# Who subtracts the low halves of twelve projection slabs: VectorE or GpSimd, with the context keys and values cut into pieces between them

## What is computed

```
hx = rmsnorm(x, g) * (1 + sc_x) + sh_x          # 512 tokens
hc = rmsnorm(ctx, g) * (1 + sc_c) + sh_c        # 256 context tokens
qx = rope(rmsnorm(hx @ wq))                     # 16 heads of 64
kx = rope(rmsnorm(hx @ wk)); vx = hx @ wv       # 4 heads of 64
kc = rmsnorm(hc @ wk);       vc = hc @ wv
p  = softmax(qx @ concat(kx, kc).T / 8);  y = (p @ concat(vx, vc)) @ wo
```

## Time and profile before

| | |
|---|---|
| median of 3 runs | 3340.39 us (3338.66 to 3344.8) |
| span of the profiled execution | 3345.0 us |
| TensorE busy | 3225.9 us, 96% |
| VectorE busy | 1487.9 us, 44% |
| ScalarE busy | 1193.4 us, 36% |
| GpSimd busy | 763.8 us, 23% |
| GpSimd low parts (L2433) | 254 instructions, 568.9 us |
| VectorE low parts (L1212) | 188 instructions, 217.5 us |

### The profile page before, as it was taken

The page is one execution under the profiler, slowest core; times in us unless marked ns, Lnnn a source line. Parts: engine busy times, 40 slices in busy tenths (PEclk is TensorE's granted clock), DMA queues, the critical chain, the costliest instruction groups (busy, mean ns, idle before and its releaser), DMA issues.

```text
span 3345.0 us, 38977 instructions
## 1 busy us (share of the span) xinstructions
PE 3225.9 (96%) x15760; PEld 2474.1 (74%) x15760; DVE 1487.9 (44%) x2166; ACT 1193.4 (36%) x1764; POOL 763.8 (23%) x399
## 2 busy tenths in 40 slices
PE   6999999999999999999999899999999979999998
PEld 4657777777665777777777576888888658868887
DVE  3572243132357114313269746223333899653234
ACT  3443234233344223423331154211112548632223
POOL 4303334434330343434310000000000039500000
PEclk9999999999999999999999999999999989999999
DMA  6413444544340455465335311222222110123322
GB/s 233 124 43 107 145 126 137 163 141 149 115 133 19 128 160 171 148 191 160 125 91 127 84 48 35 70 63 64 63 63 63 38 38 1 35 67 88 108 87 77
DMA packets 429893, 337.23 MB, mean 101 GB/s; under 512 B 16637, under 2 KB 411223, under 8 KB 417428
## 3 DMA queue, kind: packets, MB, share of 16 engines
q1 hardware_dynamic: 428272, 334.23, 32.9%
q0 software_dynamic: 1248, 0.46, 0.1%
q10 hardware_dynamic: 196, 0.07, 0.0%
HBM read 319.58 MB, written 2.10 MB: 96 GB/s over the span
## 4 chain that ended last, share of the span: by engine, by line
PE 59%; DVE 6%; ACT 2%; POOL 1%; issue 1%; SPq 0%; DMA 0%; DVEq 0%; ACTq 0%
PE PS L423 17%; PE PS L424 17%; PE PS L425 17%; PE PS L771 1%; POOL p L2478 1%; PE PS L586 1%; PE PS L512 1%; DVE both_tmp L1289 1%; PE PS L565 1%; PE PS L1075 1%; PE PS L1076 0%; PE PS L1044 0%; PE PS L1055 0%; DVE stat_r L1272 0%; DVE stat_t L1266 0%
## 5 line engine op out<-in xcount | busy, mean ns | idle before, releaser
L423 PE MATMUL PS<-Hh,Wh 128*128 128x512 f32 x2208 | 877.0, 397 | 13.7 <-DVE Hl L1303 9.4
L424 PE MATMUL PS<-Hl,Wh 128*128 128x512 f32 x2208 | 861.8, 390 | 0.0
L425 PE MATMUL PS<-Hh,Wl 128*128 128x512 f32 x2208 | 861.3, 390 | 0.0
L2433 POOL TENSOR_TENSOR Wl<-raw,Wh 128x1024 fp32r<-128x1024 f32 (+2 forms) x254 | 568.9, 2244 | 1099.3 <-ACT Wh L1950 1099.3
L1950 ACT ACTIVATE Wh<-raw 128x1024 fp32r<-128x1024 f32 (+2 forms) x442 | 436.1, 987 | 404.4 <-PE PS L425 394.2
L423 PEld LDWEIGHTS PS<-Hh,Wh 128*128 128x128 f32 x2208 | 416.0, 188 | 139.1 <-issue 74.0
L425 PEld LDWEIGHTS PS<-Hh,Wl 128*128 128x128 f32 x2208 | 415.6, 188 | 87.8
L424 PEld LDWEIGHTS PS<-Hl,Wh 128*128 128x128 f32 x2208 | 416.2, 188 | 67.2 <-issue 3.5
L1212 DVE TENSOR_TENSOR Wl<-raw,Wh 128x1024 fp32r<-128x1024 f32 (+3 forms) x188 | 217.5, 1157 | 386.2 <-ACT Wh L1950 385.7
L1858 DVE SCALAR_TENSOR_TENSOR cv<-PS,vcols,cv 128x510 f32<-128x510 f32 (+1 forms) x176 | 123.7, 745 | 295.7 <-ACT cv L2357 295.7
L423 PE MATMUL PS<-g_h,Wh 128*128 128x512 f32 x528 | 211.2, 400 | 0.0
(11 more groups left out here) (370 smaller groups left out, 4827.0 us busy)
## 6 DMA issues: line engine op xcount, KB each, us to landing
raw<-in_ffn_w SPq DMA_DIRECT2D x108, 512.0 KB, 3.8
mod_w<-in_w_mod SPq DMA_DIRECT2D x48, 1024.0 KB, 5.6
raw<-in_w_up SPq DMA_DIRECT2D x88, 512.0 KB, 3.8
mod_w<-in_w_ada SPq DMA_DIRECT2D x40, 1024.0 KB, 6.0
raw<-in_w_in SPq DMA_DIRECT2D x62, 512.0 KB, 4.1
UQ<-U SPq DMA_DIRECT2D x128, 99.4 KB, 2.2
raw<-in_w_down SPq DMA_DIRECT2D x32, 384.0 KB, 3.4
raw<-in_conv_w_pw SPq DMA_DIRECT2D x24, 512.0 KB, 4.6
```

The costliest lines, as they stand in the source:

```text
L423: pe.matmul(o, wh, xh, start=start, stop=False, skip_group_check=True)
L424: pe.matmul(o, wh, xl, start=False, stop=False, skip_group_check=True)
L425: return pe.matmul(o, wl, xh, start=False, stop=stop, skip_group_check=True)
L2433: pool.tensor_tensor(low, src, high.bitcast(F32), ALU.subtract).then_inc(*mark("w_low_pool", one[0]))
```

## The change

The jobs k2, v2 and q2 of the grouped attention join `by_pool`, so that VectorE's `ahead` skips their twelve low parts and GpSimd makes them. GpSimd's program for them is a loop over the twelve jobs. After the low part of the seventh job (q2) it waits for the new x and for the scaled context keys and makes half of the context keys, after q3's the other half, after q4's it waits for the turned values and makes half of the context values, and after q5's the other half. After each low part it waits for its own instruction. `wo2` slabs stay with VectorE.

```diff
     def by_pool(key):
-        return key[0] in BLOCK_1_SLABS or key[0:2] == ("dn", 1)
+        return key[0] in BLOCK_1_SLABS or key[0:2] == ("dn", 1) or key[0] in ("k2", "v2", "q2")
...
+        def weight_low(d):
+            one = slabs[d]
             src, high = halves(one, raw[d % RAW], Wh[d % WS])
             _, low = halves(one, raw[d % RAW], Wl[d % WS])
             pool.wait_ge(*ready("w_high", one[0]))
             pool.tensor_tensor(low, src, high.bitcast(F32), ALU.subtract).then_inc(*mark("w_low_pool", one[0]))
...
-        pool.wait_ge(*ready("x_new", ("ffn", 0, "x"), KD - 1))
-        pool.wait_ge(*ready("head_scaled", "k2", "c", KVH // 2 - 1))
-        pool.wait_ge(*free(("turned", "v2", "c", 1)))
-        for e in range(2):
+        def ctx_keys(e):
...
-        for c in range(2):
+
+        def ctx_values(c, *event):
...
+        for i, job in enumerate(attention_jobs):
+            weight_low(number[job])
+            j = i - CTX_HEADS - KVH // 2
+            pool.wait_ge(*low_ready(job))
+            if j == 0:
+                pool.wait_ge(*ready("x_new", ("ffn", 0, "x"), KD - 1))
+                pool.wait_ge(*ready("head_scaled", "k2", "c", KVH // 2 - 1))
+            if 0 <= j < 2:
+                ctx_keys(j)
+            elif j == 2:
+                pool.wait_ge(*free(("turned", "v2", "c", 1)))
+                ctx_values(0, "v_low", 0)
+            elif j == 3:
+                ctx_values(1)
```

More of the change, by code:

```diff
@@ L2426, in _ @@
             pool.dma_start(o, src).then_inc(*mark("vec_in_rest", *([i] if i + 1 < len(pieces[1]) else []), by=16))
-        for d, one in enumerate(slabs):
-            if not by_pool(one[0]):
-                break
+        def weight_low(d):
+            one = slabs[d]
             src, high = halves(one, raw[d % RAW], Wh[d % WS])
@@ L2433, in _ @@
             pool.tensor_tensor(low, src, high.bitcast(F32), ALU.subtract).then_inc(*mark("w_low_pool", one[0]))
+        number = {one[0]: d for d, one in enumerate(slabs)}
+        for d, one in enumerate(slabs):
+            if not by_pool(one[0]):
+                break
+            weight_low(d)
         w_dw = vec("w_dw", 0, TAPS * KD).rearrange("p (t j) -> p t j", j=KD)
@@ L2472, in _ @@
                 pool.wait_ge(*own(pool.tensor_copy(one[:, :, :, b, :], v), "v", c, b))
-            i = pool.tensor_tensor(one[:, :, :, 1, :], v, one[:, :, :, 0, :].bitcast(F32), ALU.subtract)
-        own(i)
+            low = pool.tensor_tensor(one[:, :, :, 1, :], v, one[:, :, :, 0, :].bitcast(F32), ALU.subtract)
+            pool.wait_ge(*own(low, *event))
+        for i, job in enumerate(attention_jobs):
[12 more added lines that the diff above has]
+                ctx_values(1)
         for n in range(G_HEADS * QT):
```

## The result

| | kernel before | kernel after |
|---|---|---|
| median of 20 runs each | 3338.77 us (3337.19 to 3355.79) | 3344.07 us (3342.47 to 3353.18) |
| ratio after / before | | 1.0017, 95% interval 1.0011 to 1.0024 |
| the same in us | | +5.7 (+3.7 to +8.0) |
| span of the profiled execution | 3345.0 us | 3341.6 us |

The changed kernel is slower by 0.17%. The two profiled spans say the opposite of the medians: the profiled execution of before had lost over 9 us ahead of the stage, where the two kernels have the same work.

The account below looks back on a forecast made before the run. VectorE, not the 96% busy TensorE, was taken to set the stage's end. Terms -0.35 - 3.4 + 1.85 + 0 + 0.5 + 9.1 + 0.4 gave +8.1, said as +8 on 3340.4: 3348.4 us, range 3343 to 3353.

Parts of the forecast that it names:

- rival C: Small loss: each meeting costs 1.48 us and v0's 1.2, so +4 us, 3344.4; chance 0.27.
- Subtractions leaving VectorE: Twelve subtractions leave VectorE: k1's returns 0.35 us, q5 to q7's 3.4 us, the others nothing.
- v0's low: On GpSimd amid VectorE's residual additions and norms: VectorE loses 2.08 us, some 0.2 absorbed, so +1.85 us.
- TensorE's first product of k0: Sign after the norms: this product would move from 2622.22 to about 2623.7 us.
- v1, q0, q1, q2 covered: Their lows on GpSimd meet VectorE, but its idle time before the rotations covers the net cost: 0 us.
- The wait on GpSimd's queue: q3's low waits behind context keys, TensorE starts q3 6 us late, mostly covered by VectorE's delay: +0.5 us.
- Meetings of q3 to q7: Where VectorE sets the pace, five GpSimd lows hold up its instructions by 1.48 to 2.08 us each: +9.1 us.
- Context parts: Same key and value instructions spread over two more blocks, more casts meeting two-operand VectorE instructions: +0.4 us.
- Rival A: TensorE becomes the bound as held-up GpSimd delays q4's and q5's lows: +12 to +14 us, 3353.5; chance 0.15.
- Rival B: Meetings cost little, lows falling beside PSUM readers and in short gaps: faster, at best -3.8 us, 3336.6; chance 0.07.
- D: The change doesn't act and VectorE still subtracts; nothing seen (0 to +1 us), chance 0.03.
- Slower by over 0.2%: Whole kernel slower by more than 6.7 us, the least a measurement can tell from no change; chance 0.61.

Follow-up runs that it names:

- e5: Kernel before with only the low parts of k0 and k1 moved to GpSimd; stage 183.79 us, ratio to before 0.9996.
- e11: Kernel after with the lows of v0 and q3 to q7 back on VectorE and context parts at the end; stage 183.87 us, ratio to before 0.9993.
- e12: Kernel after with the lows of k0 to q2 back on VectorE, only q3 to q7 on GpSimd; stage 190.42 us, ratio to before 1.0017.
- e3: Kernel after with GpSimd making the subtractions of q3 to q7 twice; stage 201.36 us, ratio to before 1.0048.
- e9: Kernel before, unchanged, profiled once more; stage 185.05 us, ratio to before 0.9998.
- e10: Kernel after, unchanged, profiled once more; stage 191.18 us, ratio to before 1.0010.
- e4: Kernel after with v0's low alone given back to VectorE; stage 189.86 us, ratio to before 1.0012.
- e8: Kernel after, lows cut to 8 of 1024 columns, two whole-tile memsets ahead of each of q3 to q7's; incomplete kernel; stage 181.10 us, ratio to before 0.9983.

## Why the prediction was nearly right

Forecast +8.1 us (3348.4), measured +5.7 (3344.07). Part of the difference in the absolute time is the start: 20 runs put before at 3338.77, 1.6 below the three that I had. The mechanism was right. By my own bands, though, +5.7 and the stage's +6.29 both fall to rival C ("small loss", +1 to +6.5, chance 0.27), just below the forecast (+6.5 to +11, 0.48). They do so only in part by C's reasons: of the short meetings that C counts on three of five came about (8.47 us in all, C has 7.4), and v0's low cost 2.09 and not 1.2. The place of the low clock, which no case had, takes another 0.6 us off. Without that my forecast band would have held, narrowly. Point by point, by the numbers of the prediction:

1. *Subtractions leaving VectorE* (-0.35 and -3.4). Right. k1's gave 0.51 (29.73 to 29.22 us at the last addition, e5). q5 to q7 give 1.14 each: block q3 of after is 8.40 = 6.97 + 1.43, one meeting and no subtraction.
2. *v0's low* (+1.85). Right mechanism, a little small: 92.15 - 90.06 = 2.09 us at k1's rotation between after and e11, both Q. L1289 took 2.58 for 0.48. I took 0.2 off for slack behind ScalarE, and there was none. One sign that I named failed: TensorE's first product of k0 did not move back but came at 2612.06 - 2551.14 = 60.92 us of the stage, where it had been at 2622.22 - 2560.70 = 61.52. Before, it stood behind TensorE's own sums at the low clock; after, it waits for VectorE (0.49 us in the row).
3. *v1, q0, q1, q2 covered* (0). Right, shown by e11: 0.08 us.
4. *The wait on GpSimd's queue* (+0.5). TensorE began q3 at 129.37 us of the stage against 124.05, so 5.3 late, I had said 6. But it was idle for only 2.34 us of it, not for the 5 to 6 that I had named as a sign; the low clock in q2 had taken part of the rest. It was hidden, all of it: L811 of q2 was done at 2688.38 + 1.02 = 2689.40, and VectorE came for it at 2691.58. The low clock after the wait was there (0.64), as forecast. The low clock in the products of q2, ahead of that wait, was not forecast: +1.60 us in q0.
5. *Meetings of q3 to q7* (+9.1). Measured after: 1.42 + 2.06 + 1.50 + 2.06 + 1.43 = 8.47 (2.10, 2.75, 2.18, 2.75, 2.12 less 0.69 or 0.68). In e12 they were 9.7. Each lies within 0.3 us of its estimate, although no low met the very instruction that I had worked out. That is in part luck: a block has only two kinds of instruction to meet, and the kind was right each time. No meeting in any run cost VectorE more than 2.1 us, so the price of the earlier trace rows was right. But I drew a wrong conclusion from it. The Trainium skill, page SBUF — State Buffer, section "Who interferes with whom", has the holder keep the shared access for the whole instruction, and I held that the hold looked shorter and that by this rule a meeting would cost 2.39. The trace agrees with the page: each held instruction of 512 columns ends 0.54 to 0.56 us after GpSimd's, in the earlier trace rows too (132.22 and 132.77, 186.83 and 187.38), and beside the casts of the earlier trace rows as well (2689.58 and 2690.13). The loss is below 2.39 because GpSimd has used a part of its time when VectorE's instruction comes, and because the held instruction then needs 0.55 us and not 0.69. L1266 lost only 0.37 because the pair of casts was nearly over: 2689.58 - 2689.07 - 0.14 = 0.37.
6. *Context parts* (+0.4). In after they cost 3.29 us in q1 to q4, in before 36.88 - 29.02 - 3.42 = 4.44, so -1.15. But most of that is the clock again. After (Q), VectorE waits 4.43 us ahead of q1's rotation, in e12 (N) 2.83, and the first keys fall into this wait. Against e5 (Q: 35.43 - 29.02 - 3.42 = 2.99) the pieces cost +0.3, as said.

The sum: at k1 -0.51 + 2.09 - 0.75 (no low clock in the norms) = +0.83; q0 +1.60; q1 to q4 -3.42 + 8.47 - 1.15 = +3.9; together 6.3 of 6.29 us. **The term that was missing** is the place of the low clock: -0.75, +1.60 and about -1.4 in the meetings with the context keys, -0.6 net. The term that was mis-sized is item 5, by 0.6, and item 4 showed nothing of its 0.5. With the low clock in the same place the change costs about 6.9, which is inside my forecast band: 7.39 above e5, less the 0.51 that e5 itself gains from k1's subtraction.

Rival A (TensorE as the bound) is refuted by the timeline after, in which VectorE is not idle from q1's rotation to the end of the stage, and by e3. Rival B (meetings cost little) and D (no effect) are refuted by the timeline: five instructions over 2 us, 176 and 266 instructions of the two lines. "Slower by over 0.2%" got 0.61 from me. The point estimate, 0.17%, is on the other side of that line, and its interval holds both sides.

What stays open is why the low clock falls in the norms in some kernels and in q2's products in others. The L512 of e9 and e10 begin at the same time behind the same idle time. What differs ahead of them is 0.5 us in the feed-forward's end, and it does not hang on this alone: e4 and e11 have the same instructions up to the norms, and are N and Q. The idle time ahead of q2's products does not tell them apart either: it is 2.71 us before, where they ran at 1.00, and 2.71 us after. I ran nothing that sets it apart. Whether it is the kernel's or chance also stays open.

## What to carry to other kernels

Before work is moved from VectorE to GpSimd, ask stretch by stretch who sets the pace: where VectorE waits for TensorE the move is free and worth nothing, and where VectorE sets the pace each of GpSimd's lows cost VectorE 1.4 to 2.1 us (for one of 2.4 us) while the subtraction that left gave back 1.14. By these numbers such a move can pay only if what GpSimd holds VectorE up for is shorter than what it relieves, if GpSimd only writes, or if its instruction can be placed in VectorE's idle time. No complete kernel here was surely faster than before. Read the durations of the neighbours, not the busy share: a held-up instruction counts as busy.

## What the runs showed of the hardware

- **The low clock has two places.** Each profiled execution of a kernel had TensorE at its lower level in one of two places of this stage. In the norms sixteen L512 took 5.98 to 6.23 us instead of 4.90, and the path lost 0.75 us (before) to 0.98 (e4 against e11). In q2's products it cost 1.6 us, of which 1.4 came back: VectorE's wait ahead of q1's rotation grew, and the first context keys fell into it. So two of these kernels can be compared to better than 1 us only if the place is the same in both.
- **GpSimd's reads hold up VectorE, its writes alone do not.** 1.97 us of memsets (e8) left L1545 at 0.68 us; a 2.7 us subtraction made it 2.18. L1544, which reads one operand from PSUM, kept its 0.69 us beside the low of 2678.01.
- **The price of a meeting is what is left of GpSimd's instruction.** The held VectorE instruction of 512 columns ends 0.54 to 0.56 us after GpSimd's. Over all kernels a low cost it 2.0 to 2.1 us if it came next after the instruction that GpSimd had waited for, 1.4 to 1.5 if one of 512 columns that reads PSUM (L1544 or L1263) went first, and 1.1 to 1.2 if the low had begun another 0.5 us earlier (v1's). GpSimd's low takes 2.46 to 2.93 us instead of 2.40 when it comes second.
